# Four heads in flight and half-width levels in a delta-rule chunk stage, with the key norm and the gates moved into the first projection

## What is computed

```python
proj = x @ w_in                                   # 512 x 4112: q, k, v, z of 8 heads x 128, then a and b
qkv = silu(causal_depthwise_conv(proj[..., :3072], conv_w))          # 4 taps
q = l2_normalize(q) * 128 ** -0.5;  k = l2_normalize(k)
g = -exp(a_log) * softplus(a + dt_bias);  beta = sigmoid(b)
o = gated_delta_rule_chunked(q, k, v, g, beta)
```

## Time and profile before

| | us |
|---|---|
| median of 3 runs | 2913.43 (2912.21 to 2916.68) |
| the profiled execution | 2917.37 |
| its span in the trace | 2915.6 |
| mean granted TensorE clock | 0.92 of full |

### The profile page before, as it was taken

The page is one execution under the profiler, slowest core; times in us unless marked ns, Lnnn a source line. Parts: engine busy times, 40 slices in busy tenths (PEclk is TensorE's granted clock), DMA queues, the critical chain, the costliest instruction groups (busy, mean ns, idle before and its releaser), DMA issues. The chain is left out here.

```text
span 2915.6 us, 34741 instructions
## 1 busy us (share of the span) xinstructions
PE 2500.4 (86%) x13054; PEld 1953.1 (67%) x13054; DVE 1265.9 (43%) x2608; ACT 978.3 (34%) x1577; POOL 742.8 (25%) x204
## 2 busy tenths in 40 slices
PE   6996788877995696899799388979999888989998
PEld 4773777756773485567677265857887746768886
DVE  3533555445545323776554536143222453243122
ACT  2333111223552111673455225152322333343222
POOL 2430000042343231001334220413543301324441
PEclk8997889977997796999899698999999999999999
DMA  4251000015885233111688331213432302223321
GB/s 107 90 209 41 1 1 1 30 45 168 277 281 184 65 101 118 64 39 45 218 282 280 131 90 38 94 54 96 131 100 72 109 27 66 81 84 102 103 85 65
DMA packets 225098, 304.41 MB, mean 104 GB/s; under 512 B 52304, under 2 KB 139872, under 8 KB 224944
## 3 DMA queue, kind: packets, MB, share of 16 engines
q1 hardware_dynamic: 222656, 294.16, 31.3%
q0 software_dynamic: 2304, 8.39, 0.8%
HBM read 270.95 MB, written 31.56 MB: 104 GB/s over the span
## 5 line engine op out<-in xcount | busy, mean ns | idle before, releaser
L159 POOL TENSOR_TENSOR branch_weights_wl<-branch_weights_wf,branch_weights_wh 128x2048 fp32r<-128x2048 f32 (+1 forms) x66 | 303.9, 4604 | 770.2 <-ACT branch_weights_wh L153 770.2
L153 ACT ACTIVATE branch_weights_wh<-branch_weights_wf 128x2048 fp32r<-128x2048 f32 (+1 forms) x66 | 125.0, 1895 | 405.8 <-PE bprojc_acc L201 133.0
L201 PE MATMUL merge_acc<-xh,branch_weights_wh 128*128 128x512 f32 x384 | 151.4, 394 | 2.9 <-PEq L72 2.9
L201 PE MATMUL merge_acc<-xh,branch_weights_wl 128*128 128x512 f32 x384 | 150.3, 391 | 0.0
L201 PE MATMUL merge_acc<-xl,branch_weights_wh 128*128 128x512 f32 x384 | 149.5, 389 | 0.0
L159 POOL TENSOR_TENSOR nsa_weights_wl<-nsa_weights_wf,nsa_weights_wh 128x2048 fp32r<-128x2048 f32 x13 | 59.7, 4594 | 275.3 <-ACT nsa_weights_wh L153 275.3
L1556 PE MATMUL exp_ps_y<-rt_wf,exp_ht 128*128 128x512 f32 x256 | 117.2, 601 | 3.9 <-ACT exp_ht L1600 3.9
L1410 POOL TENSOR_TENSOR rt_wl<-rt_wf,rt_wh 128x2048 fp32r<-128x2048 f32 x16 | 82.6, 5163 | 128.9 <-ACT rt_wh L1406 128.9
L159 POOL TENSOR_TENSOR in_weights_wl<-in_weights_wf,in_weights_wh 128x2048 fp32r<-128x2048 f32 x16 | 75.3, 4709 | 129.1 <-ACT in_weights_wh L153 110.6
L201 PE MATMUL gproj_acc<-xh,in_weights_wh 128*128 128x512 f32 x256 | 100.8, 394 | 3.7 <-POOL in_weights_wl L159 3.7
L201 PE MATMUL gproj_acc<-xh,in_weights_wl 128*128 128x512 f32 x256 | 100.5, 393 | 0.0
(11 more groups left out here) (612 smaller groups left out, 6705.0 us busy)
## 6 DMA issues: line engine op xcount, KB each, us to landing
branch_weights_wf<-w_in SPq DMA_DIRECT2D x56, 1024.0 KB, 5.0
rt_wf<-moe_w_down SPq DMA_DIRECT2D x32, 1024.0 KB, 5.5
in_weights_wf<-gdn_w_in SPq DMA_DIRECT2D x16, 1024.0 KB, 5.6
rt_wf<-moe_w_gate SPq DMA_DIRECT2D x32, 512.0 KB, 7.4
rt_wf<-moe_w_up SPq DMA_DIRECT2D x32, 512.0 KB, 8.2
moe_rows<-rt_y SPq DMA_DIRECT2D x64, 256.0 KB, 2.1
moe_rows<-gproj_zeros SPq DMA_DIRECT2D x1, 12288.0 KB, 35.7
merge_bwf<-w_branch SPq DMA_DIRECT2D x12, 1024.0 KB, 5.0
```

The costliest lines, as they stand in the source:

```text
L153: act.activation(self.h[u][:, :, 0:self.cols(b)], self.s.f[u][:, :, 0:self.cols(b)], ACT.Copy).then_inc(self.s.hi_ready, 1)
L159: pool.tensor_tensor(self.l[u][:, :, 0:self.cols(b)], self.s.f[u][:, :, 0:self.cols(b)], self.h[u][:, :, 0:self.cols(b)].bitcast(F32), ALU ...
L201: mm = pe.matmul(self.acc[:, s, 0:cols], lhs[:, P * s:P * s + P], rhs, start=(u == 0 and k == 0 and n == 0), stop=(u == 1 and k == HALF - ...
```

## The change

The two stages gnorm and ggate are gone; their instructions are issued inside the projection, between those of blocks 4 to 7. In the chunk stage four heads are in flight, two rounds, with two banks and four tiles a head, and a level works on the halves that it changes. The masks of levels 1 to 6 are transposed on the host.

```diff
 # WeightRun.multiply: after(u, s) is called behind each group of 12 matmuls
+                if after:
+                    after(u, s)
...
 # class KeyNorm (new)
+    def load(self, sp, a):
+        sp.wait_ge(self.summed, self.N)
+        sp.dma_start(self.sel, a["c_sel"]).then_inc(self.loaded, 16)
+    def squares(self, act, r0):
+        if r0:
+            act.wait_ge(self.summed, r0)
+        for r in range(r0, r0 + 8):
+            act.activation(self.sq[:, r % 8, :], self.qkvz[:, r, :], ACT.Square).then_inc(self.squared, 1)
+    def invert(self, dve):
+        dve.wait_ge(self.loaded, 16)
+        dve.tensor_copy(self.g.sel[:], self.sel).then_inc(self.sel_ready, 1)
+        dve.wait_ge(self.rooted, 1)
+        link = Link(dve, self.step)
+        link(dve.reciprocal(self.inv, self.root))
+        link(dve.tensor_copy(self.invh[:], self.inv))
+        dve.tensor_tensor(self.invl[:], self.inv, self.invh[:].bitcast(F32), ALU.subtract).then_inc(self.inverted, 1)
+    def spread(self, pe, r):
+        if r == 0:
+            pe.wait_ge(self.inverted, 1)
+            pe.wait_ge(self.sel_ready, 1)
+        if r >= 2:
+            pe.wait_ge(self.used, r - 1)
...
 # stage_gdn_project: SyncE
                 ws.load_rest(sp)
+                gates.load(sp, a)
+                norm.load(sp, a)
 # the store of zeros, now from a tile of half the width
+                for c in range(2):
+                    sp.dma_start(g.moe_rows[:, 512 * c:512 * c + 512].rearrange("(b p) d -> p b d", p=P),
...
 # TensorE
+                over(pe, 4, lambda b: ws.multiply(pe, b, g.xh, g.xl, True))
+                def beside(b):
+                    def after(u, s):
+                        if b < 6 and u == 1:
+                            for r in range(2):
+                                norm.sum(pe, 8 * (b - 4) + 2 * s + r)
+                        elif b == 6 and u == 1 or b == 7 and u == 0:
+                            for r in range(2):
+                                norm.spread(pe, 8 * (b - 6) + 2 * s + r)
+                        if b == 6 and u == 1 and s == 3:
+                            gates.sums(pe, ab_done)
...
 # ScalarE
+                for b in (4, 5):
+                    act.wait_ge(silu_done, 2 * GDN_H)
+                    norm.squares(act, 8 * (b - 4))
+                    conv_block(b)
                 for b in (6, 7):
                     if b == 6:
+                        norm.roots(act)
+                        gates.softplus(act, ab_done)
                         ws.hi(act, 7, 0)
+                    else:
+                        gates.exponentials(act)
...
 # VectorE, behind its conv_block(5)
+                gates.magnitude(dve, ab_done)
+                norm.invert(dve)
+                gates.decay_and_beta(dve)
+                for row in range(8):
+                    norm.scale(dve, row)
+                gates.take_sums(dve)
...
 # stage_gdn_chunks, TensorE: a level (lv) of head i
+                def off(i, r, lv):
+                    dve_did.wait(pe, i, r, "lower" if lv == 1 else f"lower{lv - 1}")
+                    for c in range(TT):
+                        mm = pe.matmul(halves(bank(i, 0, c), lv, 0), B[i]["at"][:, c, :], halves(B[i]["tm"][:, c, :], lv, 0),
+                def grow(i, r, lv):
+                    dve_did.wait(pe, i, r, f"off{lv}")
+                    if lv < L:
+                        for c in range(TT):
+                            pe.matmul(compact(ps[i][:, 1, 64 * c:64 * c + 64], lv), b["um"][:, c, :],
+                                      halves(b["x"][:, c, :], lv, 0), start=True, stop=True)
+                    for c in range(TT):
+                        mm = pe.matmul(compact(ps[i][:, 1, 256 + 64 * c:256 + 64 * c + 64], lv), b["x"][:, c, :],
+                                       halves(b["um"][:, c, :], lv, 1), start=True, stop=True)
...
+                for r in range(GDN_H // NB):
+                    for i in range(NB):
+                        decay(NB * r + i, i, r)
+                        gram(NB * r + i, i, r)
+                    for i in range(NB):
+                        beta(NB * r + i, i, r)
+                    for i in range(NB):
+                        score(NB * r + i, i, r)
+                    for i in range(NB):
+                        first(i, r)
+                    for lv in range(1, L + 1):
+                        for i in range(NB):
+                            off(i, r, lv)
+                        for i in range(NB):
+                            grow(i, r, lv)
+                    for i in range(NB):
+                        turned(NB * r + i, i, r)
+                    for i in range(NB):
+                        new(i, r)
...
 # VectorE, a head's products behind the scores, and a level
+                def score(h, i, r):
+                    dve_did.done(dve.tensor_tensor(qk_t[:, h, :], flat(b["x"][:]), ps[i][:, 0, :], ALU.mult), i)
+                    dve_did.done(dve.tensor_tensor(q, q, flat(b["um"][:]), ALU.mult), i)
+                    dve_did.done(dve.tensor_tensor(b["x"][:], b["at"][:], spread(levels[:, 0, :]), ALU.mult), i)
+                    dve_did.wait(dve, i, r, "first")
+                    dve_did.done(dve.tensor_tensor(b["um"][:], spread(g.ident[:]), b["x"][:], ALU.subtract), i)
+                def off(i, r, lv):
+                    dve_did.done(dve.tensor_tensor(B[i]["x"][:], wide(ps[i][:, 0, :]), spread(levels[:, lv, :]), ALU.mult), i)
+                def grow(i, r, lv):
+                    if lv < L:
+                        low = chunk_halves(b["tm"][:], lv, 0)
+                        dve_did.done(dve.tensor_tensor(low, low, compact(ps[i][:, 1, 0:256], lv), ALU.subtract), i)
+                    up = chunk_halves(b["um"][:], lv, 1)
+                    dve_did.done(dve.tensor_tensor(up, up, compact(ps[i][:, 1, 256:512], lv), ALU.subtract), i)
```

More of the change, by code:

```diff
@@ L417, in conv_block @@
                             ins.then_inc(step if j < 3 else conv_done, 1)
[L418 to L475, removed]
-                    dve.wait_ge(spread_done, r + 1)
-                    dve.scalar_tensor_tensor(qkvz[:, r, :], qkvz[:, r, :],
-                                             P ** -0.5 if r < GDN_H else 1.0, spread[:, r % 4, :],
-                                             ALU.mult, ALU.mult).then_inc(used, 1)
@@ new lines, in _, with __init__, done, wait @@
+                over(dve, 4, conv_block)
+                for b in (4, 5):
+                    conv_block(b)
+                gates.magnitude(dve, ab_done)
[4 more added lines that the diff above has]
+                gates.take_sums(dve)
+                for row in range(8, 16):
+                    norm.scale(dve, row)
+                gates.finish(dve)
+class Steps:
+    def __init__(self, sems, names):
+        self.sems, self.names = sems, names
+    def done(self, ins, i):
+        ins.then_inc(self.sems[i], 1)
+    def wait(self, eng, i, r, name):
+        eng.wait_ge(self.sems[i], len(self.names) * r + self.names.index(name) + 1)
+    def wait_round(self, eng, i, r):
+        if r:
+            eng.wait_ge(self.sems[i], len(self.names) * r)
@@ L564, in stage_gdn_chunks @@
         ld = st.sem("loaded")
-        pe_done = [st.sem(f"pe_done{i}") for i in range(NB)]
-        act_done = [st.sem(f"act_done{i}") for i in range(NB)]
-        dve_done = [st.sem(f"dve_done{i}") for i in range(NB)]
-        L = LEVELS - 1
-        N_PE, N_ACT, N_DVE = 6 + (3 * L - 1) + 1, 9 + L, 8 + (3 * L - 1) + 2
+        pe_did = Steps([st.sem(f"pe_done{i}") for i in range(NB)],
+                       ["decay", "gram", "beta", "score", "first"]
+                       + [f"{x}{lv}" for lv in range(1, L + 1) for x in ("off", "grow")]
+                       + ["turn_k", "turn_v", "new_v", "new_k"])
@@ L572, in flat, with wide @@
+        act_did = Steps([st.sem(f"act_done{i}") for i in range(NB)], ["growth", "decay", "k_beta", "v_beta", "new_k"])
+        dve_did = Steps([st.sem(f"dve_done{i}") for i in range(NB)],
+                        ["mask", "dec_beta", "at", "score", "query", "first", "upper", "lower"]
+                        + [f"{x}{lv}" for lv in range(1, L + 1) for x in (("off", "lower", "upper") if lv < L else ("off", "upper"))]
+                        + ["k_dec", "new_v"])
         def flat(ap):
             return ap.rearrange("p c n -> p (c n)")
+        def wide(ap):
+            return ap.rearrange("p (c n) -> p c n", c=TT)
@@ L594, in front, with gram, beta @@
                                        start=True, stop=True)
-                    mm.then_inc(pe_done[i], 1)
+                    pe_did.done(mm, i)
+                def gram(h, i, r):
+                    dve_did.wait_round(pe, i, r)
+                    for c in range(TT):
+                        kc = qkvz[:, GDN_H + h, P * c:P * c + P]
+                        mm = pe.matmul(bank(i, 1, c), kc, kc, start=True, stop=True)
+                    pe_did.done(mm, i)
+                def beta(h, i, r):
```

(9 more changed lines are left out.)

408 lines of the change are left out of this document (203 added, 205 removed).

## The result

The changed kernel takes 2952.65 us (median of 4, 2948.6 to 2953.68) where the kernel before, on the same chip, takes 2913.56 (2912.21 to 2916.68): ratio 1.0118, 95% interval 1.0105 to 1.0132. (The ratio is the one on record; the two medians divided give 1.0134, 39.1 us.) The forecast was 2945.8 us, the slower case with both level loops at half clock. The profiled execution took 2952.77 us, with a span of 2951.0.

The account below looks back on a forecast made before the run. TensorE was taken to bound projection and level loops: chunks start at 254.9, two rounds of 158.4 end at 571.7, 32.3 us later; 2917.4 becomes 2949.7, less 3.9 for the median: 2945.8 us, range 2815 to 2965.

Parts of the forecast that it names:

- the slower case: Chunk stage: both rounds' level loops at half clock, 2945.8 us, own range 2930 to 2962; chance 54%.
- The clock step: Chunk stage: clock falls in each `first` phase, doesn't rise in the 64-column loop (0.2133 us a record), rises in `new`.
- Loop and records: Level loop of a round: 544 records paced by the weight load, 60.7 us at full clock, 116.0 at half.
- Stall in block 6: Projection, term (c): TensorE waits 8.8 us for the inverse, plus 2.5 us lost to the clock, 11.3 in all.
- Start of the chunks: First chunk matmul: terms sum to 255.6, block lengths give 254.2, taken as 254.9, 19.3 us earlier than 274.2.
- (a): Projection, blocks 4 and 5: 16 column sums at 0.876 us each add 14.0 us on TensorE.
- (b): Projection: 32 spreading matmuls of 512 columns at 0.23 us add 7.3 us, four small records 0.45 us.
- the GpSimd waits: Projection, blocks 5 and 6: two waits of 1.2 us fall away, of which 1.5 us is counted.
- The barrier: Between last block matmul and first chunk matmul, term (d): 2.0 us, 0.7 for the last eviction and 1.3 more.
- the zeros: Behind the projection: the 3.9 us pause that waited for the zeros falls away.
- Fronts and tails: Each chunk round at the forecast clock: front 26 us, tail 16.4; at full clock the tail is 12.4.
- a mere shift: Behind the chunk stage: everything untouched, shifting with the stage's end, 32.3 us later.

Follow-up runs that it names:

- the burst: Changed kernel with twenty unread matmuls of 128 columns ahead of the grow products of level 3 in each round: 2896.42 us, ratio 0.9924.
- the early loads: Changed kernel with gate vectors and selection rows loaded ahead of the weights, selection cast at the start: executions 2886.1, 2943.5, 2928.7 and 2877.3 us, no ratio.
- the pauses filled: Changed kernel with unread 128-column matmuls put into the pauses of `first`, 64 columns kept in the level loops: 2836.28 us, ratio 0.9726.

## Why the prediction came true, and where its terms were off

**The clock step.** The range, 2815 to 2965 us, took in faster kernels and slower ones, and the slower case had 54%, so that the time lies in it says little; the mechanism is what can be held against the runs. The forecast was made at one point, the granted clock with which `off` of level 1 begins, and both halves of it stand. That the pauses of `first` bring the clock down: with them filled or shortened it stays at 1.00. That 64 columns don't raise it again: 128 columns do in 4 us, 64 don't in 116, and a burst of 128 does. What I had left open, whether 64 columns hold a clock that is up, is answered by every kernel that entered a loop with it, that with the burst and that with the early loads among them: they do. The Trainium skill, "TensorE: Matmul & The Clock Gate", section "Why this matters for your kernels", names long idle gaps between bursts as what costs the clock. It does not say that shorter ones are harmless, and here they were not: the clock fell behind idle times of 1.08 and three times 1.37 us, and did not behind 0.58 and three times 0.17.

**Loop and records.** 115.95 us measured in each round for a forecast of 116.0; at full clock 60.69 for 60.7. That the weight load sets the pace is a reading: PEld is busy for all of each loop, and 64 columns have the pace of 128. No run varied the load itself. The same page of the Trainium skill, section "Step-by-step: what each phase is for", says that a matmul's time follows the number of moving columns; for f32 with a new 128x128 stationary operand for each matmul the trace differs, 0.1116 us a record with 64 columns as with 128.

**Stall in block 6.** 8.81 us for 8.8, and with the clock 11.0 for 11.3. The two causes named, the loads queued behind the last weight load and the cast held beside GpSimd, went together when the loads were moved, so their shares were not told apart. The Trainium skill, "SBUF — State Buffer", section "Terms", has VectorE and GpSimd sharing a pair of ports that one of them holds for a whole instruction; the trace agrees: 4.03 us beside the low part, 0.42 without it.

**Start of the chunks: 254.9 forecast, 259.41 measured.** Terms (a) and (b) were undersized: each change between block matmuls and narrow ones costs TensorE some 0.1 us more than the pace, on the way in and on the way back. From the early loads, where there is no stall, a pair of column sums and a group of four spreading matmuls with their neighbours:
```profile
154.89 0.39 PE L201 MATMUL gproj_acc<-xh,in_weights_wl 128*128 128x512 f32 x1
155.21 1.89 PE L352 MATMUL gproj_narrow<-gproj_sq,colsel 128*16 128x512 f32 x4
157.03 0.51 PE L201 MATMUL gproj_acc<-xh,in_weights_wh 128*128 128x512 f32 x1
157.37 0.40 PE L201 MATMUL gproj_acc<-xl,in_weights_wh 128*128 128x512 f32 x1
...
205.60 0.39 PE L201 MATMUL gproj_acc<-xh,in_weights_wl 128*128 128x512 f32 x1
205.92 0.50 PE L376 MATMUL gproj_spread<-gproj_invh,sel 16*128 16x512 f32 x1
...
207.03 0.50 PE L201 MATMUL gproj_acc<-xh,in_weights_wh 128*128 128x512 f32 x1
207.37 0.39 PE L201 MATMUL gproj_acc<-xl,in_weights_wh 128*128 128x512 f32 x1
```
Two steps between block matmuls are 0.46 us. A pair of sums adds 2.48 - 0.46 = 2.02, forecast 1.75; a spreading group adds 1.77 - 0.46 = 1.31, forecast 0.92. Eight of each: 2.2 + 3.1 = 5.3 us. I had taken 0.7 less than the sum gave. The other way go 0.3 for the stall, 0.3 since the GpSimd waits that fell away were 1.8 us and not 1.5, and 1.3 since the first block matmul started that much sooner in this profile. These make 4.1 of the 4.5. The barrier took the 2.0 forecast (the last block matmul ends at 257.43), with no pause behind the zeros.

**Fronts and tails.** Fronts 26.7 and 25.0 us for 26. The tail was over-sized: 12.8 us for 16.4, since the clock rises already in the transposes, 4.3 us in, and not in `new`, and since ScalarE's scalings don't hold TensorE (with the clock up the tail is 10.9 us, 347.30 to 358.24, for 12.4). The stage took 309 us for 316.8.

**Sum.** Start +4.5, stage -7.6: its end is 29.2 us later than before, for 32.3. Behind it I had forecast a mere shift, and 6.2 us more came: the barrier was 0.7 shorter, then the 6.9 above, which lie within the spread of that code. Together that is 3.1, the 2952.8 of the profiled execution for 2949.7. The other 3.8 up to the 6.9 of the median come from the step from one to the other: the execution of before that was profiled lay 3.9 above its median, this one 0.1. So the clock step was foreseen, but that the total came within 7 us is in part luck: a start 4.5 us later than forecast stands against a stage 7.6 us shorter.

## What to carry to other kernels

More tiles in flight and fewer columns moved both looked like gains. The new stage does gain at full clock: 196 us with the pauses filled (261.35 to 457.43), where the old one took 268 with its own falls of the clock; what four heads give of that and what VectorE's halved work gives, no run tells apart. But on TensorE this loop of f32 matmuls, each with a new stationary operand, took 0.1116 us a record with 128 columns and with 64, so halving the columns saved nothing there and took away what brings the clock back. Look at the granted clock where such a loop begins, and at the pauses of a microsecond just ahead of it: here moving two VectorE products a head out of them, with no work removed, turned 1.2% slower into 3.1% faster.

## What was not expected

Useless work made the kernel faster: 44 matmuls that nobody reads, 114 us. A clock that falls sooner can be the better one: in the second round of the early loads it fell two `first` groups sooner than in the changed kernel's first, the slower groups shortened the pauses, and it was back before the loop. Executions of that kernel lay 66 us apart. And a VectorE step of 32 elements took 4.62 us beside GpSimd's low part.
